# Chunk-causal encoder step on one core: x normalised and transposed ahead of the adaLN product, which is split between VectorE and TensorE

## What is computed

```
mod = silu(c) @ ada_w + ada_b            # c: 2 vectors (prompt, sample); ada_w: 1024 x 6144
sh1, sc1, g1, sh2, sc2, g2 = six pieces of 1024 of mod
h  = rmsnorm(x, norm1_w) * (1 + sc1) + sh1
z  = h @ w_in + b_in                     # w_in: 1024 x 3080
ya = rglru(...z...); yb = mlstm(...z...)
x  = x + g1 * (concat(ya, yb) @ w_out)
h2 = rmsnorm(x, norm2_w) * (1 + sc2) + sh2
x  = x + g2 * peer(h2, ...)              # top-16 of 16384 experts per head, 8 heads, gathered rows
y  = rmsnorm(x, final_norm_w)
```

## Time and profile before

| | |
|---|---|
| median of 3 runs | 3436.58 us (3435.76 to 3439.36) |
| the profiled execution's own time | 3432.43 us |
| its span | 3430.6 us |
| mean granted TensorE clock | 0.972 |
| PE busy | 2951.0 us (86%) |
| DVE busy | 2232.9 us (65%) |
| ACT busy | 2153.9 us (63%) |
| head, to the end of the first z block | about 78 us |

### The profile page before, as it was taken

The page is one execution under the profiler, slowest core; times in us unless marked ns, Lnnn a source line. Parts: engine busy times, 40 slices in busy tenths (PEclk is TensorE's granted clock), DMA queues, the critical chain, the costliest instruction groups (busy, mean ns, idle before and its releaser), DMA issues. The chain is left out here.

```text
span 3430.6 us, 41834 instructions
## 1 busy us (share of the span) xinstructions
PE 2951.0 (86%) x9150; PEld 1412.7 (41%) x9150; DVE 2232.9 (65%) x5470; ACT 2153.9 (63%) x7233; POOL 1207.8 (35%) x1127
## 2 busy tenths in 40 slices
PE   7999999968888888898888888888888888888876
PEld 3555445534333443343334433443444343334321
DVE  3664526566667666666766676666666766676765
ACT  3232114357777777777677777777677777777775
POOL 0000100034444444444444444444344444444443
PEclk9999989989999999999999999999999999999999
DMA  6222031299999999999999999999999999999998
GB/s 240 105 74 73 23 108 51 103 417 412 420 419 413 397 419 419 414 398 419 398 417 402 419 416 416 399 419 392 419 405 419 406 400 419 419 414 399 420 420 336
DMA packets 167931, 1190.39 MB, mean 347 GB/s; under 512 B 19466, under 2 KB 19594, under 8 KB 28402
## 3 DMA queue, kind: packets, MB, share of 16 engines
q0 software_dynamic: 155584, 1118.66, 79.5%
q1 hardware_dynamic: 12084, 68.95, 5.3%
HBM read 1178.27 MB, written 9.25 MB: 346 GB/s over the span
## 5 line engine op out<-in xcount | busy, mean ns | idle before, releaser
L833 PE MATMUL ps<-r_w,r_yT 128*128 128x512 f32 (+1 forms) x3168 | 1524.9, 616 | 321.8 <-ACT r_yT L1130 314.6
L1648 DVE SCALAR_TENSOR_TENSOR r_yT<-r_w,r_qk 128x1024 bf16<-128x1024 f32 x792 | 969.0, 1225 | 684.1 <-DMA r_w<-in_peer_uv,gidx 674.9
L560 POOL DMA_INDIRECT r_w<-in_peer_uv,gidx x792 | 877.7, 1108 | 994.2 <-PE ps L833 835.7
L833 PEld LDWEIGHTS ps<-r_w,r_yT 128*128 128x128 f32 (+1 forms) x3168 | 553.5, 189 | 1209.5 <-issue 1208.2
L833 PE MATMUL ps<-r_yT 128*128 128x512 f32 (+1 forms) x1056 | 524.1, 631 | 102.7 <-ACT r_yT L1130 91.8
L1122 ACT ACTIVATE mixc<-mixc 128x1 f32<-128x1 f32 x1056 | 207.2, 196 | 455.5 <-DVE r_yT L1648 450.8
L560 POOL DMA_INDIRECT r_yT<-in_peer_uv,gidx x264 | 291.9, 1106 | 557.0 <-PE ps L833 495.1
L1130 ACT ACTIVATE r_yT<-ident,mixc 128x128 f32<-128x128 f32 x1024 | 411.2, 402 | 93.5
L1126 ACT ACTIVATE mixc<-mixc 128x1 f32<-128x1 f32 x1056 | 409.2, 387 | 35.0
L1125 ACT ACTIVATE mixc<-mixc 128x1 f32<-128x1 f32 x1056 | 408.3, 387 | 33.8
L1648 DVE SCALAR_TENSOR_TENSOR r_yT<-r_yT,r_qk 128x1024 bf16<-128x1024 f32 x264 | 322.9, 1225 | 117.2 <-DMA r_yT<-in_peer_uv,gidx 95.3
(11 more groups left out here) (282 smaller groups left out, 2380.9 us busy)
## 6 DMA issues: line engine op xcount, KB each, us to landing
r_w<-in_ada_w SPq DMA_DIRECT2D x16, 1024.0 KB, 5.1
r_w<-in_peer_uv,gidx POOLq DMA_INDIRECT x792
r_w<-in_w_lin SPq DMA_DIRECT2D x16, 512.0 KB, 10.8
r_w<-in_ada_w SPq DMA_DIRECT2D x3, 2048.0 KB, 17.3
r_yT<-in_peer_uv,gidx POOLq DMA_INDIRECT x264
r_vo<-in_x_prompt SPq DMA_DIRECT2D x8, 512.0 KB, 18.6
r_w<-in_w_vo SPq DMA_DIRECT2D x2, 2048.0 KB, 8.0
r_w<-in_w_out SPq DMA_DIRECT2D x1, 4096.0 KB, 14.2
```

The source lines that it names most:

```text
L560: pool.indirect_dma_start(ring[place(h, j)], None, table, bass.IndirectOffsetOnAxis(gidx_t[:, h, j:j + 1], 0))\
L833: mm = nc.tensor.matmul(ps[0:r, 2 * p + c, :], diag[:, j % 4, 0:r], row[:, D + c * 512:D + (c + 1) * 512], start=h == 0 and j == 0, stop=h ...
L1648: V.scalar_tensor_tensor(udump[j % 2], ring[i][:, 0:D], 1.0, h2[:, t, :], ALU.mult, ALU.mult, accum_out=dots[:, i:i + 1]).then_inc(dot_don ...
```

## The change

- x comes first on SP, all nine tiles, ahead of any adaLN weight. Square sums, roots and scaling are done in three groups of three tiles.
- All nine tiles are transposed at once, ahead of the adaLN product, and copied plainly out of PSUM, one instruction of 4x128 columns a tile and engine. The factor and the shift are applied afterwards, in place in `hT`, by depth slices of 128: k = 2 and 5 on ACT, the other six on DVE. The first z group waits for one slice after the other (`h_modd`, `h_moda`).
- adaLN blocks 2 and 3 become sums on DVE, by `ada_part`, as the later blocks are. PE sums `acc` over the partitions by `early_sum`, 8 matmuls with a stationary 128x128 piece and one moving column of ones.
- adaLN blocks 0 and 1 stay on PE, but with the weights as the stationary operand and silu(c) as the moving one: `early_block`, 32 matmuls of 128x128 weights and two moving columns a block. The results come out as columns, so that the 16 small transposes and the four `mod_row` go.
- Block 3 of the weights uses the buffers of block 2, so its two loads wait on SP for `half_done`; the loads of block 1 and of the first eight z blocks stand behind them.
- POOL's three early loads wait for the first `early_sum`.
- The bias of blocks 0 to 3 comes with the parameters as 16 more columns (`adaT`, `N_PRM` 162 to 178).

```diff
+            for t in range(NT):
+                sp.dma_start(xin[0:rows(t), t, :], x_rows[t]).then_inc(ld_x[t // 3], 16)
+            def load_half(b, i):
+                if b >= 3:
+                    sp.wait_ge(half_done[i], b - 2)
+                sp.dma_start(ada_half[i], w[:, 4 * i:4 * i + 4, :]).then_inc(half_ld[i], 16)
...
+            load_half(2, 0)
+            load_half(2, 1)
+            load_early(0)
+            load_half(3, 0)
+            load_half(3, 1)
+            load_early(1)
             for i in range(8):
                 load_z(i)
...
+            pool.wait_ge(ada_mm, 1)
             pool.dma_start(kTt[:, :, :], A["peer_kT"]).then_inc(kt_ld, 16)
...
+            def early_block(b):
+                for c in range(4):
+                    if c % 2 == 0:
+                        pe.wait_ge(ada_ld[b][c // 2], 16)
+                    for k in range(KD):
+                        nc.tensor.matmul(early_column(b, c), ada[b][:, c, k, :], csil[:, :, k], start=k == 0, stop=k == KD - 1)
+            def early_sum(b):
+                pe.wait_ge(half_done[1], b - 1)
+                for c in range(4):
+                    for s in range(2):
+                        m = nc.tensor.matmul(early_column(b, c, s), acc[s][:, c * P:(c + 1) * P], ones[:, 0:1], start=True, stop=True)
+                m.then_inc(ada_mm, 1)
...
+            for t in range(NT):
+                turn_x(t)
+            pe.wait_ge(c_silu, 1)
+            early_block(0)
+            early_sum(2)
+            early_block(1)
+            early_sum(3)
+            pe.wait_ge(x_evd, NT)
+            pe.wait_ge(x_eva, NT)
...
                     for k in range(KD):
+                        if nblk == 0 and g == 0:
+                            pe.wait_ge(h_moda if k % 3 == 2 else h_modd, k // 3 + 1 if k % 3 == 2 else k - k // 3 + 1)
...
+            squares(0)
+            x_root(0)
+            squares(1)
+            x_root(1)
+            for t in range(3):
+                evict_x(t)
+            squares(2)
+            x_root(2)
+            for t in range(3, NT):
+                evict_x(t)
...
+            x_scale(0)
+            x_scale(1)
+            for t in range(3):
+                evict_x(t)
+            x_scale(2)
+            for t in range(3, NT):
+                evict_x(t)
+            dve.wait_ge(c_silu, 1)
+            ada_part(2)
+            ada_part(3)
+            dve.wait_ge(ada_mm, 2)
+            link(V.tensor_tensor(modT, ps[:, 2, 0:32].rearrange("p (a k s) -> p a k s", a=2, s=2),
+                                 adaT.unsqueeze(3).broadcast_to([P, 2, KD, 2]), ALU.add))
...
+            for k in (0, 1, 3, 4, 6, 7):
+                for s, c in ((0, slice(0, SEQ)), (1, slice(SEQ, T))):
+                    m = V.tensor_scalar(hT[:, k, c], hT[:, k, c], mul1[:, s, k:k + 1], modT[:, 0, k, s:s + 1], ALU.mult, ALU.add)
+                m.then_inc(h_modd, 1)
```

More of the change, by code:

```diff
@@ L569, in _, with early_column @@
         def _(pe):
[L570 to L576, removed]
+            def early_column(b, c, s=None):
+                return ps[:, 2, b * 8 + 2 * c:b * 8 + 2 * c + 2] if s is None else ps[:, 2, b * 8 + 2 * c + s:b * 8 + 2 * c + s + 1]
+            def early_block(b):
[9 more added lines that the diff above has]
+                        m = nc.tensor.matmul(early_column(b, c, s), acc[s][:, c * P:(c + 1) * P], ones[:, 0:1], start=True, stop=True)
                 m.then_inc(ada_mm, 1)
             def ada_sum(b):
-                pe.wait_ge(half_done[1], b - 3)
-                pe.wait_ge(mod_ev, b)
+                pe.wait_ge(half_done[1], b - 1)
+                if b >= 5:
+                    pe.wait_ge(mod_ev, b - 4)
                 for s in range(2):
@@ L880, in _ @@
             act.wait_ge(consts, 1)
-            for t in range(NT):
-                r = rows(t)
-                if t % 3 == 0:
-                    act.wait_ge(ld_x[t // 3], 48)
-                if t:
-                    act.wait_ge(x_sq, t)
-                nc.scalar.activation(sq_junk[0:r], xin[0:r, t, :], ACT.Square, accum_out=ssq[0:r, t:t + 1]).then_inc(x_sq, 1)
-            act.wait_ge(x_sq, NT + 1)
-            nc.scalar.activation(ssq, ssq, ACT.Sqrt).then_inc(x_rt, 1)
-            act.wait_ge(mul1_ready, 1)
@@ L891, in _, with squares, x_root @@
-            for t in range(NT):
+            def squares(g):
+                act.wait_ge(ld_x[g], 48)
+                for t in range(3 * g, 3 * g + 3):
+                    r = rows(t)
+                    if t:
+                        act.wait_ge(x_sq, t)
+                    nc.scalar.activation(sq_junk[0:r], xin[0:r, t, :], ACT.Square, accum_out=ssq[0:r, t:t + 1]).then_inc(x_sq, 1)
+            def x_root(g):
+                act.wait_ge(x_var, g + 1)
+                c = slice(3 * g, 3 * g + 3)
+                nc.scalar.activation(ssq[:, c], ssq[:, c], ACT.Sqrt).then_inc(x_rt, 1)
@@ new lines, in _ @@
+            squares(0)
[8 more added lines that the diff above has]
+                evict_x(t)
+            act.wait_ge(mul1_ready, 1)
+            act.wait_ge(x_evd, NT)
+            act.wait_ge(x_eva, NT)
+            for k in (2, 5):
+                for s, c in ((0, slice(0, SEQ)), (1, slice(SEQ, T))):
+                    m = nc.scalar.activation(hT[:, k, c], hT[:, k, c], ACT.Identity, scale=mul1[:, s, k:k + 1],
+                                             bias=modT[:, 0, k, s:s + 1])
+                m.then_inc(h_moda, 1)
@@ L1208, in _, with x_scale @@
-            dve.wait_ge(mul1_ready, 1)
-            def evict_x(t):
-                r, s = rows(t), stream(t)
+            def x_scale(g):
+                c = slice(3 * g, 3 * g + 3)
+                dve.wait_ge(x_sq, 3 * g + 3)
+                V.tensor_scalar(ssq[:, c], ssq[:, c], 1.0 / D, EPS, ALU.mult, ALU.add).then_inc(x_var, 1)
+                dve.wait_ge(x_rt, g + 1)
+                link(V.reciprocal(rstd1[:, c], ssq[:, c]))
+                for t in range(3 * g, 3 * g + 3):
+                    r = rows(t)
+                    V.tensor_scalar(xin[0:r, t, :], xin[0:r, t, :], rstd1[0:r, t:t + 1], None, ALU.mult).then_inc(x_sc, 1)
@@ L1225, in ada_part @@
             def ada_part(b):
-                dve.wait_ge(ada_mm, b)
+                if b >= 3:
+                    dve.wait_ge(ada_mm, b - 2)
                 for k in range(KD):
```

128 lines of the change are left out of this document (46 added, 82 removed).

## The result

The change is slower by 0.22%. The median of its 16 runs is 3445.68 us (3442.75 to 3448.46, and one disturbed execution of 6077.4, which the ratio leaves out), that of 16 runs of the kernel before 3438.48 us (3435.02 to 3440.94). The ratio is 1.0022, with an interval of 1.0015 to 1.0030, which is +7.2 us within 5.2 and 10.3.

A forecast was written before the change was run, and what follows sets the result against it. PE was taken as the bound, so the first z block's end, moving from 78.3 to 91.7 us, shifts the whole time: 3436.6 + 13.4 = 3450.0 us, range 3437 to 3455.

The forecast's parts named there:

- The mechanism: Head: PE's early blocks run at low clock, 0.22 us a record, and DVE waits for PE; +13.4 us, chance 0.57.
- x: Start of the head: first three x tiles land at 8.9 us instead of 16.48; DVE is free at 37.
- my two cases: Head transposes: a tile takes 1.0 us at full clock or 1.8 at half; DVE free at 34 or 37.
- Block 0: First early adaLN block on PE: 64 records at 0.22 us, 14.1 us, from 37 to 51.1.
- The row that I took as nearest: Kernel before, 488 to 508 us: matmuls of 128 and 129 columns and transposes stayed at clock 0.50.
- the rival that kept loads at full pace: Early blocks on PE: low clock slows only the moving side; blocks take 7.5 us; +6.3, 3443 us; chance 0.13.
- DVE's part 3: DVE's second early sum, for block 3: 11.0 us straight behind part 2, from 48 to 59.
- Block 1: Second early adaLN block on PE: starts when its load lands at 55.8 us, takes 14.1, ends at 69.9.
- sum 3: PE's early_sum of block 3, behind block 1: 3.5 us, ending at 73.4.
- The first z block: End of the head: PE starts at 75.3, first group ends at 82.6, other two take 9.1; 91.7 against 78.3.
- against 78.3: Base for the head: end of the first z block in the kernel before, 78.3 us, giving +13.4.
- step one for one: Whole kernel: a shift of the first z block's end shifts the total time equally, as everything behind hangs on PE.

The follow-up runs named there:

- three narrow blocks: The three-and-one order with two moving columns instead of 128 in its three PE blocks; one execution, 3446.96 us, marker 116.47.
- second profile of before: The kernel before, unchanged, profiled once more in one execution; span 3438.2 us, marker 109.92 against 106.81 in the first profile.
- three-and-one order: Against the change: adaLN blocks 0, 1, 2 on PE with 128 moving columns, only block 3 on DVE, loads reordered; 3427.29 us, ratio 0.9972 to before.

## Why the prediction was right, and where it was off

The forecast was 3450.0 in a range of 3437 to 3455, slower by over 0.2% with the highest chance. The change came out at 3445.7, +7.2, which is slower by just over that bound. The mechanism is the one forecast: PE's narrow rows at the low clock, with block 1 behind the waits on SP, and DVE waiting for PE (9.72 us) and not PE for DVE. The size, +13.4 where +7.2 was measured, was too large. That the miss against 3450.0 is 4.3 only is luck: the median of before came out 1.9 above the one that I started from. By its own steps:

- **x.** The first squares came at 8.3 (8.9 forecast), DVE's last plain copy ended at 35.2 (34 to 37, 37 taken). The transposes ran at 0.50 at 22 to 24 and from 28 to 34 us, and at 0.93 behind it, between my two cases. The first 16, at 14.43, took 3.29, or 0.21 each, the pace of the low level, although the row says 1.00 there.
- **Block 0** took 11.5 where 14.1 was forecast. The price at 1.2 GHz was right, 0.22 a record; what I missed is that it would begin at the high level. It gained nothing for the end, since PE then waited for block 1's load. The row that I took as nearest, 488 to 508 us, had shown work of 128 columns staying at 0.50; the windows at 34 to 38 and the run with three narrow blocks show that a run of 128-column transposes can bring the clock up. Why the clock came up there and stayed down at 488 to 508, where short pauses stood between the rows of matmuls (three, of 0.78 to 0.93 us, at 493, 502 and 505), no run shows. The Trainium skill, "TensorE: Matmul & The Clock Gate", Part 4, says that transposes don't engage the full clock; the trace disagrees here, with 0.50 and then 0.93 under them, and in the three narrow blocks with 0.50 and then 1.00. By that rule the block would have taken my 14.1.
- **The load rate.** 19 records in 2 us at 0.93 against 20 in 4 us at 0.50 decide against the rival that kept loads at full pace. The Trainium skill, same page, section "LDWEIGHTS (loading the stationary operand)", gives a load as its columns over 1.2 without regard to the clock; the spacing of 0.105 to 0.117 us here agrees with it at the high level, and that of 0.20 to 0.22 at the low one does not.
- **DVE's part 3** ended at 61.2, not 59. I had it start straight behind part 2 and overlooked that it waits for `early_sum(2)` to have read `acc`: 3.99 us. It cost nothing, as PE was later still, and that too is luck; in the version with 128 columns and the load ahead it is what bound.
- **Block 1** 53.54 to 67.35 (55.8 to 69.9), sum 3 to 70.8 (73.4), factors 71.5 (74.2), first z matmul 72.7 (75.3): all early because the load landed 2.3 us sooner than forecast. It stands behind DVE's part 2, which ended at 46.2 and not at 48, as DVE was free at 35.2 and not at 37. PE waited 3.60 for it where I had put 1.2, so that even a block 0 of 14.1 would have been done before it.
- **The first z block** ended at 90.0 (91.7). From its first matmul to its end it took 17.3 where I had 16.4; the clock was at 0.67 still from 76 to 80.

That gives +11.7 for the first block's end against the profile of before, where the forecast had +13.4. The other part of the miss is a **base that was one good execution**: I set the new head against 78.3 us, read from one profile whose 3432.43 us lay below all 16 of its runs. In the second profile of before the head was 3.1 us longer, for the clock in its second and third group. With markers of 106.81 and 109.92 for before and 117.69 and 118.43 for the change, the shift of the head is 7.8 to 11.6, and the medians say 7.2 and 8.9. So two terms of the sum were mis-sized: the first, "against 78.3", by up to 3 us, and the time at which DVE is free, 37 for 35.2, with the load behind it (2.3 together, of which the slower first z block takes 0.9 back). Which of its two heads the kernel before has more often, two profiles don't show. The step one for one held as far as single executions can tell: in the two first profiles the shift is 11.6 at the first adaLN sum and 13.1 at the end of the span, and behind the marker the two profiles of before differ by 4.5 us and those of the change by 1.1. I can't attribute the last 2 or 3 us more finely than that.

Where the head's time went, by the runs: making the PE work wide takes 7.6 us off the marker, moving the load 5.8, but both together only 6.7, as the chain through DVE lies right behind. With a block moved from DVE to PE and all of it wide, 20 us go. With that order and narrow matmuls hardly 2 do. The clock is the larger cause, though not the only one: the three-and-one order is ahead of the kernel before with the clock up, and no better than the change without it; but without the new order the wide or moving weights alone didn't bring the version ahead of before (1.0015 with the weights moving, 0.9999 with 128 columns and the load ahead).

## What to carry to other kernels

A matmul with a big stationary operand and one or two moving columns is not cheap because it has few columns. Here a record took 0.10 to 0.12 us at the high level whether 2 or 128 columns moved, and in every block of 64 narrow records TensorE's clock fell or stayed low while the profile shows it fully busy, for itself and for the first work behind it. If such a form is wanted, try the moving operand repeated to 128 columns, which cost PE nothing here, and read the granted clock: at 488 to 508 us of the kernel before work of 128 and 129 columns with short pauses stayed at 0.50. Or leave the weights moving. And where a head is judged by a few us, take the base from several executions, and look at the granted clock in its pauses before taking one as the typical one.

## What was not expected of the hardware

- More work was faster. 64 records took 7.41 us with 128 moving columns, 9.34 with 32 and 11.46 with 2 in the first block, and 9.04, 13.86 and 13.81 in the second, which began at a clock of 0.50 in all three.
- The granted clock fell while PE was busy without a gap (the change, 0.93 at 36 to 38 us and 0.50 at 38 to 40), and stood at 1.00 in a window in which PE was busy 1.54 of 4.00 us (the second profile of before, at 60). Busy time doesn't tell the clock.
- Under a run of 128-column transposes the clock rose from 0.50 to 1.00 (35.0 to 41.6 us in the three narrow blocks).
- Behind a narrow sum and a pause of 2.5 us the first three z blocks took 45.24 us, and with both filled by wide matmuls 43.06 (one execution each).
